# An expert loop whose passes pack several experts into one tile: two passes of three experts become one of two and one of four, which stands last

## The chip, the core and the metric

The kernel runs on one core of one Trainium2 chip. The metric is the device time of one execution in microseconds; the shown times are three runs of the same kernel. A profile of one further execution was taken by the hardware profiler.

## What is computed

The reference is one inference step of a small trunk of two layers over 128 context tokens and 128 sample tokens, 256 in all, each of width 1024, in float32. Each layer has a mixer (layer 0 a bidirectional linear recurrence, layer 1 differential attention) and then a mixture of 64 experts, of which each token takes 8. An expert is three matrices, gate and up of 1024 x 256 and down of 256 x 1024, 1 MB each. Only the mixture matters here:

```python
scores = jax.nn.sigmoid(x @ router)                     # (tokens, 64)
combine = ...                                           # top 8 of 64, 0 for the others
h = jax.nn.silu(jnp.einsum('btd,edf->btef', x, w_gate)) * jnp.einsum('btd,edf->btef', x, w_up)
routed = jnp.einsum('btef,efd->btd', h * combine[..., None], w_down)
shared = (jax.nn.silu(x @ ws_gate) * (x @ ws_up)) @ ws_down
return routed + shared
```

## The kernel before

**Passes.** All 64 experts of a layer are loaded, and the tokens that chose an expert are gathered for it. One pass of TensorE handles 128 gathered token slots, which are four lanes of 32. The string `ORDER` (line 54) says how the 26 passes of a loop split their lanes, and `SUBS` (line 59) which lane belongs to which expert of the pass. In a pass A two experts have two lanes each, in a pass B three experts have two, one and one, in a pass D two experts have three and one. The experts of a layer are numbered 0 to 63 in the order in which the passes consume them; `FIRST` (line 60) holds the first number of each pass. Experts 0 to 5 are fixed, the others are ordered on the chip by how many tokens they have, so that those with more tokens fall on more lanes; `column_ranks` (line 69) makes the table for that. What doesn't fit an expert's lanes is done by extra items, after pass 17.

**One pass** (`one_pass`, line 1387). TensorE does the gate and up products (`pass_gate_up`, or two halves one after the other in the first passes and in the last one), the scatter of the pass before, the transposes of the hidden rows, the gather for the pass after, the down product and the turning of the slots. All matmuls go through the helper `mm` and have its line, 889, in the profile. ScalarE takes the SiLU of the gate half (line 1872) when the gate and up products are done. VectorE and ScalarE copy between them. The gate and up products of a pass with lanes of 64 issue half as many matmuls as those with lanes of 32.

**Buffers.** SBUF has six places for a gate and up pair (`GATE_SLOTS`) and five for a down matrix (`DOWN_SLOTS`), line 49. Expert n uses the place `gate_of(n)` (line 468, in turns of six from expert 5 on) and the place n mod 5 for its down matrix. A place is refilled as soon as the expert that used it is done: `GATES_FREED` and `DOWNS_FREED` (lines 477 and 479) list, for each pass, the later experts whose place it frees.

**Loads.** SyncE issues them all, into one queue, in the order of its program. `refill(L, p)` (line 595) waits until the gate and up products of pass p are done (`gu_done`), issues the gate and up loads of the experts that take over its gate places, waits until the down product is done (`down_done`) and issues the down loads. The experts of the last pass, `END_EXPERTS` (line 481), are an exception: first the gate halves of all of them are issued, on the semaphore `end_gate_loaded`, then the up halves on the place's own semaphore (lines 615 to 622). In the last pass (line 1392) TensorE waits for all gate halves, does the gate half of the products, waits for the up halves and does the other half. Its wait counts `END_PLACES` (line 65), the gate places of the last pass. After the refills SyncE issues the load of the residual's gains and then, behind the first loop, the weights of the next stage.

**The end of the loop before the change**, with numbers of experts:

| pass | kind | experts | gate and up loads it sets free | down loads it sets free |
|---|---|---|---|---|
| 16 | B | 39, 40, 41 | 45, 46, 47 | 44, 45, 46 |
| 17 | A | 42, 43 | 48, 49 | 47, 48 |
| 22 | D | 54, 55 | 60, 61 | 59, 60 |
| 23 | A | 56, 57 | 62, 63 | 61, 62 |
| 24 | B | 58, 59, 60 | none | 63 |
| 25 | B | 61, 62, 63 | none | none |

The rest of a layer's mixture (the routing and its plan, the shared expert, the residual) is not touched. The first layer has no extra item in this run, the second has one, between passes 17 and 18.

Of the kernel before, what the change touches and what calls it, by code (L numbers as in the profile page):

```python
# [33 lines left out]
D = 1024  # L34
# [13 lines left out]
RING = 4  # L48
# [2 lines left out]
DOWN_LOADS = (E - RING) // DOWN_SLOTS + 1  # L51
STATIC = GATE_SLOTS
PLACED = RING + 1
ORDER = "AA" + "BABABDBA" + "BABABDBA" + "BABADABB"
ROUND = 8
PASSES = len(ORDER)
COLS = 4 * PASSES
ITEMS = COLS + 2 * XITEMS
SUBS = {"A": (0, 0, 1, 1), "B": (0, 0, 1, 2), "D": (0, 0, 0, 1)}
FIRST = [sum(SUBS[q][-1] + 1 for q in ORDER[:p]) for p in range(PASSES)]  # L60

SHARED_GATE, SHARED_UP, SHARED_DOWN = 4, 8, (12, 14)
MIDDLE = PASSES - ROUND
HALVED, EXTRAS = 5, 5
END_PLACES = (RING + 1, 2, 3)
FIRST_HALVES = 4

def column_ranks():

    n_big = ORDER.count("D")
    n_mid = ORDER.count("B") + 2 * ORDER.count("A") - STATIC
    big = iter(range(STATIC, STATIC + n_big))
    mid = itertools.chain(range(STATIC), range(STATIC + n_big, E))
    small = iter(range(STATIC + n_big + n_mid, E))
    lanes = []
    for kind in ORDER:
        if kind == "A":
            lanes.append([(next(mid), 2), (next(mid), 2)])
        elif kind == "B":  # L80
            lanes.append([(next(mid), 2), (next(small), 1), (next(small), 1)])
        else:
            lanes.append([(next(big), 3), (next(small), 1)])
    return [(rank, block) for places in lanes for rank, blocks in places for block in range(blocks)]
# [46 lines left out]
def constants():  # L131

    c = np.zeros((P, C_N), np.float32)
    c[:, C_ID:C_ID + P] = np.eye(P)
    c[:, C_TRI:C_TRI + P] = np.triu(np.ones((P, P)))
    c[:, C_ONE:C_ONE + P] = 1.0
    c[:, C_IOTA:C_IOTA + 64] = np.arange(64)
    c[:, C_E] = np.arange(P)
    c[:, C_EPS] = EPS
    for i in range(NS * MOD_MOST):  # L140
        c[i::32, C_SEL + i] = 1.0
    for i, (rank, block) in enumerate(column_ranks()):
        c[:, C_RANK + i], c[:, C_PLACE + i] = rank, -1.0 - 32 * block
    c[:, C_KEY] = E - 1 - np.arange(P)
    c[0:STATIC, C_KEY] = 1e5 * (STATIC - np.arange(STATIC))
    c[:, C_STEP:C_STEP + 4] = SLOTS * np.arange(4)
    pairs = HD // 4
    freqs = (10000.0 ** (-np.arange(pairs, dtype=np.float32) / pairs)).astype(np.float32)
    t = np.arange(P)
    ar = (t // 64).astype(np.float32)[:, None] * freqs  # L150
    ac = (t % 64).astype(np.float32)[:, None] * freqs
    c[:, C_COS:C_COS + HD] = np.concatenate([np.cos(ar), np.cos(ar), np.cos(ac), np.cos(ac)], 1)
    c[:, C_SIN:C_SIN + HD] = np.concatenate([-np.sin(ar), np.sin(ar), -np.sin(ac), np.sin(ac)], 1)
    return c
# [46 lines left out]
def slot_value(n):  # L201

    start = 48 * [q for _, q in PROLOGUE].count(n % RING)
    expert = [e for n0 in N_EXPERT for e in range(n0, n0 + RING * GATE_LOADS)]
    halved = [n0 + RING * (GATE_LOADS - 1) + q for n0 in N_EXPERT for q in END_PLACES if q < RING] + \
        list(range(N_EXPERT[1], N_EXPERT[1] + FIRST_HALVES))
    whole = tuple(range(N_QKV, N_QKV + 6)) + tuple(range(N_WO, N_WO + 4))
    return start + sum(16 if m in halved else 32 if m in expert else 48 if m in whole else 0 for m in range(n % RING, n + 1, RING))  # L210

def trunk(nc, a, outs, gains):
    y_prompt, y_sample, new_state, new_k, new_v = outs
    ctx = ExitStack()
    with ctx:
# [241 lines left out]
        def experts_of(p):  # L458
            return list(range(FIRST[p], FIRST[p] + SUBS[ORDER[p]][-1] + 1))

        def id_column(n):

            p = max(p for p in range(PASSES) if FIRST[p] <= n)
            return 4 * p + SUBS[ORDER[p]].index(n - FIRST[p])

# [31 lines left out]
        def gate_value(L, q, times):  # L497
            if q < RING:
                return slot_value(N_EXPERT[L] + q) + 32 * times
            return 32 * ((GATE_LOADS - 1) * L + times + 1) - 16 * L * (q in END_PLACES)  # L500

        def lanes(p, place_of):

            kind = ORDER[p]
            cut = (0, 64, 128) if kind == "A" else (0, 32, 64, 96, 128)
            return [(lo, hi - lo, place_of(experts_of(p)[SUBS[kind][lo // 32]])) for lo, hi in zip(cut, cut[1:])]

# [379 lines left out]
        def _(eng):  # L887
# [290 lines left out]
            def half_gate_up(j, half, places, done, within=None):  # L1178

                for k in range(KD):  # L1180
                    for lo, n, q in places:
                        at = 2048 * half + F * k
                        ins = mm(PS[lo:lo + n, 6, F * half:F * (half + 1)], xg[:, k, lo:lo + n],
                                 gate_place(q)[:, at:at + F], k == 0, k == KD - 1)
                    if within and k == 3:
                        within()
                if done:
                    ins.then_inc(done, 1)
# [48 lines left out]
            def moe(L):  # L1237
# [149 lines left out]
                def one_pass(p):  # L1387
# [4 lines left out]
                    if not more:  # L1392
                        eng.wait_ge(s.xg_act, j + 1)
                        eng.wait_ge(s.xg_dve, j + 1)
                        eng.wait_ge(s.end_gate_loaded, 16 * len(END_PLACES) * (L + 1) + 16)
                        half_gate_up(j, 0, lanes(p, gate_of), None)
# [1430 lines left out]
```

## Time and profile before

| | |
|---|---|
| three runs | 1354.79, 1354.95, 1357.23 us; median 1354.95 |
| the profiled execution | 1353.37 us, of which the span 1351.5 |
| TensorE matmul busy | 1293.1 us, 96% of the span |
| VectorE, ScalarE busy | 463.6 us (34%), 344.5 us (25%) |
| bytes moved by DMA | 507.94 MB, 376 GB/s over the span |
| chain of work that ended last | TensorE 87%, DMA 5%, VectorE 4%, ScalarE 2% |
| granted TensorE clock, mean | 0.988 |

### The profile page before, as it was taken

What the parts mean: (1) busy time and instruction counts of PE and PEld (TensorE: products, weight loads), DVE (VectorE), ACT (ScalarE), POOL (GpSimd) and SP (SyncE); (2) the same over time, 40 slices, a digit from 0 to 9 for tenths busy, and PEclk for the clock granted to TensorE, in tenths of its full rate; (3) what the DMA queues carried; (4) which work ended last, traced back from release to release, by engine and by line L of the source; (5) the groups of instructions that cost most, each with busy time, mean ns of one, the idle gap of its engine ahead of it and who ended that gap; (6) DMA issues with size and microseconds to landing.
All of it is one profiled execution on the core that took longest, in us unless ns stands there. A gap on an engine that the chain in (4) does not pass through costs nothing.

```text
span 1351.5 us, 24835 instructions
## 1 busy us (share of the span) xinstructions
PE 1293.1 (96%) x10046; PEld 682.7 (51%) x10046; DVE 463.6 (34%) x1188; ACT 344.5 (25%) x712; POOL 18.2 (1%) x23
## 2 busy tenths in 40 slices
PE   7989998999999999899989999899999999979997
PEld 5757646565454443344534454565645444444443
DVE  2556625323232223222231253632232322222223
ACT  2168033212212212122230243522121212212222
POOL 2100000000000000000000000000000000000000
PEclk9999999999999999899999999999999999999999
DMA  9896899999999999999999556889999999999996
GB/s 346 225 351 244 326 373 414 368 419 413 420 420 421 420 420 420 419 421 419 415 391 341 201 212 263 316 345 422 413 419 421 420 420 420 421 420 419 420 420 250
DMA packets 114514, 507.94 MB, mean 376 GB/s; under 512 B 19036, under 2 KB 27424, under 8 KB 64352
## 3 DMA queue, kind: packets, MB, share of 16 engines
q1 hardware_dynamic: 113136, 503.42, 92.8%
q0 software_dynamic: 1008, 2.45, 0.6%
q8 instruction: 83, 1.36, 0.4%
q10 hardware_dynamic: 256, 0.45, 0.1%
q14 instruction: 31, 0.25, 0.0%
HBM read 504.15 MB, written 2.14 MB: 375 GB/s over the span
## 4 chain that ended last, share of the span: by engine, by line
PE 87%; DMA 5%; DVE 4%; ACT 2%; issue 1%; SPq 0%; DVEq 0%; ACTq 0%
PE PS L889 84%; DMA W<-in_moe_w_up 2%; DMA ring<-in_moe_w_up 2%; DVE W L2262 1%; DMA ring<-in_mod_w 1%; PE PS L1194 1%; DMA ring<-in_moe_w_down 1%; PE PS L897 1%; DVE x L2137 0%; PE PS L1282 0%; DVE hT L2097 0%; PE PS L1521 0%; ACT W L1831 0%; ACT W L1830 0%; DVE W L2259 0%
## 5 line engine op out<-in xcount | busy, mean ns | idle before, releaser
L889 PE MATMUL PS<-ring,W 128*32 128x512 f32 (+5 forms) x3176 | 600.4, 537 | 1.5 <-DMA ring<-in_moe_w_down 0.8
L889 PE MATMUL PS<-W 128*128 128x128 bf16 (+7 forms) x3466 | 555.8, 360 | 4.6 <-DVE ring L2270 2.3
L889 PEld LDWEIGHTS PS<-W 128*128 128x128 bf16 (+4 forms) x3466 | 257.8, 110 | 129.7 <-issue 105.9
L889 PEld LDWEIGHTS PS<-ring,W 128*32 128x32 f32 (+2 forms) x3176 | 202.2, 121 | 196.3 <-issue 173.7
L889 PE MATMUL PS<-W,junk 128*128 128x128 bf16 x848 | 117.6, 221 | 7.3 <-issue 4.0
L889 PE MATMUL PS<-diag,W 128*128 128x512 bf16 (+2 forms) x424 | 114.8, 399 | 4.8 <-ACT diag L1887 2.2
L2393 DVE TENSOR_TENSOR diag<-PS,diag 128x512 f32<-128x512 f32 x100 | 69.1, 691 | 144.4 <-ACT diag L1885 144.4
L2387 DVE COPY W<-PS 128x512 f32<-128x512 f32 x53 | 36.6, 691 | 238.6 <-PE PS L889 238.6
L889 PE MATMUL PS<-ring,hT 128*128 128x512 f32 x256 | 115.5, 601 | 0.4 <-ACT hT L2028 0.3
L1885 ACT CAST diag<-PS 128x512 bf16<-128x512 f32 x100 | 58.5, 585 | 190.8 <-PE PS L889 190.8
L2370 DVE SCALAR_TENSOR_TENSOR W<-W,PS 128x256 f32<-128x256 f32 x52 | 25.0, 480 | 217.0 <-ACT W L1872 217.0
L1872 ACT ACTIVATE W<-PS 128x256 f32<-128x256 f32 x52 | 19.9, 383 | 287.4 <-PE PS L889 287.4
L889 PEld LDWEIGHTS PS<-W,junk 128*128 128x128 bf16 x848 | 67.1, 98 | 19.5 <-issue 6.9
L889 PE MATMUL PS<-hT,ring 128*128 128x256 f32 x320 | 73.5, 389 | 2.2 <-DVE hT L2097 2.2
L889 PEld LDWEIGHTS PS<-diag,W 128*128 128x128 bf16 (+2 forms) x424 | 38.8, 103 | 73.0 <-issue 46.3
L889 PEld LDWEIGHTS PS<-ring,hT 128*128 128x128 f32 x256 | 47.4, 192 | 55.4 <-issue 54.6
L889 PEld LDWEIGHTS PS<-hT,ring 128*128 128x128 f32 x320 | 61.1, 194 | 16.7 <-issue 5.9
L1880 ACT COPY W<-PS 128x512 f32<-128x512 f32 x53 | 31.1, 586 | 142.4 <-PE PS L889 142.4
L2398 DVE TENSOR_TENSOR rows<-diag 128x1024 bf16<-128x1024 f32 x50 | 61.3, 1226 | 9.6 <-ACT diag L1887 8.4
L1887 ACT CAST diag<-diag 128x1024 bf16<-128x1024 f32 x50 | 52.3, 1046 | 37.9 <-DVE diag L2393 37.9
L889 PE MATMUL PS<-rows,W 128*128 128x512 bf16 x200 | 60.4, 384 | 1.0 <-DVE rows L2398 1.0
L889 PE MATMUL PS<-ring,condT 128*32 128x512 f32 (+1 forms) x400 | 43.9, 564 | 0.2 <-DMA ring<-in_mod_w 0.2
(284 smaller groups left out, 858.0 us busy)
## 6 DMA issues: line engine op xcount, KB each, us to landing
ring<-in_moe_w_down SPq DMA_DIRECT2D x104, 1024.0 KB, 19.6
ring<-in_moe_w_gate SPq DMA_DIRECT2D x88, 1024.0 KB, 17.5
ring<-in_moe_w_up SPq DMA_DIRECT2D x88, 1024.0 KB, 20.8
W<-in_moe_w_gate SPq DMA_DIRECT2D x40, 1024.0 KB, 16.3
W<-in_moe_w_up SPq DMA_DIRECT2D x40, 1024.0 KB, 19.5
W<-in_moe_w_down SPq DMA_DIRECT2D x25, 1024.0 KB, 17.9
ring<-in_mod_w SPq DMA_DIRECT2D x28, 768.0 KB, 9.0
ring<-in_mod_w SPq DMA_DIRECT2D x16, 1024.0 KB, 12.2
```

Source lines behind the costliest of these rows:

```text
L889: return eng.matmul(out, lhsT, rhs, start=first, stop=last, skip_group_check=True)
L897: ins = eng.transpose(PS[:, norm_bank(n, b), i * P:(i + 1) * P], junk2[:, st, k * P:(k + 1) * P], ident)
L1194: ins = eng.transpose(PS[:, 7, fc * P:(fc + 1) * P], hE[:, fc * P:(fc + 1) * P], ident)
L1872: eng.activation(sg, PS[:, 6, 0:F], ACT.Silu).then_inc(sg_.silu_ready, 1)
L1880: eng.copy(xg[:, 0:4, :].rearrange("p k n -> p (k n)"), PS[:, 6, :]).then_inc(sg_.xg_act, 1)
L1885: eng.copy(oparts[0][:, half * 512:(half + 1) * 512], PS[:, 4 + half, :]).then_inc(sg_.o_act, 1)
L1887: eng.copy(oparts[1], orest).then_inc(sg_.o_act, 1)
L2262: ins = eng.scalar_tensor_tensor(out=y, in0=xpad[:, c, :, t:t + P], scalar=conv_w(t, c), in1=y, op0=ALU.mult, op1=ALU.add)
L2370: eng.scalar_tensor_tensor(out=hE.rearrange("p (c q) -> p c q", c=2), in0=sg.rearrange("p (q c) -> p c q", c=2), scalar=wslot[:, 0:1], in1 ...
L2387: eng.tensor_copy(xg[:, 4:8, :].rearrange("p k n -> p (k n)"), PS[:, 7, :]).then_inc(sg_.xg_dve, 1)
L2393: eng.tensor_tensor(orest[:, cols], PS[:, 4 + half, :], oparts[0][:, cols], ALU.subtract)\
L2398: eng.tensor_tensor(oparts[2], orest, oparts[1], ALU.subtract).then_inc(sg_.o_dve, 1)
```

## The change

The order of a loop changes at two passes: pass 16 goes from B to A, the last pass 25 from B to a new kind C with one expert for each lane. The table of ranks and the list of the last pass's gate places follow.

```diff
-ORDER = "AA" + "BABABDBA" + "BABABDBA" + "BABADABB"
+ORDER = "AA" + "BABABDBA" + "BABABDAA" + "BABADABC"
...
-SUBS = {"A": (0, 0, 1, 1), "B": (0, 0, 1, 2), "D": (0, 0, 0, 1)}
+SUBS = {"A": (0, 0, 1, 1), "B": (0, 0, 1, 2), "D": (0, 0, 0, 1), "C": (0, 1, 2, 3)}
...
-END_PLACES = (RING + 1, 2, 3)
+END_PLACES = (1, RING + 1, 2, 3)
...
             lanes.append([(next(mid), 2), (next(small), 1), (next(small), 1)])
+        elif kind == "C":
+            lanes.append([(next(small), 1) for _ in range(4)])
```

Each expert from number 41 on moves to a later place in the passes, and with it the loads that it sets free:

| pass | kind | experts | gate and up loads it sets free | down loads it sets free |
|---|---|---|---|---|
| 16 | A | 39, 40 | 45, 46 | 44, 45 |
| 17 | A | 41, 42 | 47, 48 | 46, 47 |
| 22 | D | 53, 54 | 59, 60 | 58, 59 |
| 23 | A | 55, 56 | 61, 62 | 60, 61 |
| 24 | B | 57, 58, 59 | 63 | 62, 63 |
| 25 | C | 60, 61, 62, 63 | none | none |

The numbers of passes, lanes, matrices and bytes are the same.

## Rows read from the trace of the kernel before

**Rows 1.** The page: DMA rate in 40 slices of the span, about 34 us each.
```profile
GB/s 346 225 351 244 326 373 414 368 419 413 420 420 421 420 420 420 419 421 419 415 391 341 201 212 263 316 345 422 413 419 421 420 420 420 421 420 419 420 420 250
```
**Rows 2.** The chain in order of time, first loop: start us, us, what.
```profile
626.10 25.41 DMA ring<-in_moe_w_up
```
**Rows 3.** Busy time in windows of one pass: length, engines busy, clock, DMA share, GB/s.
```profile
641.90:658.80 16.90, 16.57 (x147) 7.77 (x148) 4.98 (x11) 3.58 (x7) 0.00 (x0) 1.00 1.01 421
1163.60:1180.50 16.90, 16.44 (x131) 7.84 (x130) 4.98 (x11) 3.56 (x6) 0.00 (x0) 1.00 1.01 419
1301.20:1317.70 16.50, 16.50 (x147) 7.37 (x148) 4.98 (x11) 3.56 (x7) 0.00 (x0) 1.00 1.01 420
```
**Rows 4.** Timeline of ScalarE: SiLU of passes 24, 25 (first layer), 24 (second).
```profile
658.78 0.38 ACT L1872 ACTIVATE W<-PS 128x256 f32<-128x256 f32 x1 [5.27 <-PE PS L889]
675.25 0.38 ACT L1872 ACTIVATE W<-PS 128x256 f32<-128x256 f32 x1 [4.90 <-PE PS L889]
...
1317.69 0.38 ACT L1872 ACTIVATE W<-PS 128x256 f32<-128x256 f32 x1 [4.89 <-PE PS L889]
```
**Rows 5.** Line 586, first layer, pass 23's four half loads: issues and time to landing.
```profile
L586 SPq DMA_DIRECT2D ring<-in_moe_w_gate x2: 333/335/337, 642.1 to 642.6; - x2
...
L586 SPq DMA_DIRECT2D ring<-in_moe_w_up x2: 377/2331/4285, 643.0 to 643.5; - x2
...
DMA to landing us min/median/max: 20.2/24.8/27.9
```
**Rows 6.** Line 579, first layer, the last three down loads (652.7, 653.3, 668.7).
```profile
L579 SPq DMA_DIRECT2D ring<-in_moe_w_down x3: 332/338/346, 652.7 to 668.7; - x3
...
DMA to landing us min/median/max: 10.1/21.1/23.1
```
**Rows 7.** Line 579, second layer, the last three down loads (1311.7, 1312.2, 1327.6).
```profile
L579 SPq DMA_DIRECT2D ring<-in_moe_w_down x3: 332/332/333, 1311.7 to 1327.6; - x3
...
DMA to landing us min/median/max: 8.9/19.9/21.9
```
**Rows 8.** Timeline of TensorE, pass 25 in both layers: first gate product, down product.
```profile
668.08 0.41 PE L889 MATMUL PS<-ring,W 128*32 128x256 f32 x2
...
678.93 3.64 PE L889 MATMUL PS<-ring,W 128*32 128x512 f32 x32 [0.84 <-DMA ring<-in_moe_w_down]
...
1326.98 0.41 PE L889 MATMUL PS<-ring,W 128*32 128x256 f32 x2
...
1336.93 3.64 PE L889 MATMUL PS<-ring,W 128*32 128x512 f32 x32
```
**Rows 9.** Line 579, pass 17's last down load in the first and second layer.
```profile
L579 SPq DMA_DIRECT2D ring<-in_moe_w_down x1: 4952/4952/4952, 541.9 to 541.9; - x1
...
DMA to landing us min/median/max: 28.6/28.6/28.6
...
L579 SPq DMA_DIRECT2D ring<-in_moe_w_down x1: 333/333/333, 1200.6 to 1200.6; - x1
...
DMA to landing us min/median/max: 27.7/27.7/27.7
```
**Rows 10.** Timeline of SyncE: pass 18's first load in both layers.
```profile
560.75 0.34 SPq L576 DMA_DIRECT2D ring<-in_moe_w_gate  x1
...
1220.06 0.33 SPq L576 DMA_DIRECT2D ring<-in_moe_w_gate  x1
```
**Rows 11.** DMA issues outside the loops: count, KB each, median us to landing.
```profile
ring<-in_attn_w_o SPq DMA_DIRECT2D x4, 512.0 KB, 3.6
...
out<-x SPq DMA_DIRECT2D x2, 512.0 KB, 2.6
```
**Rows 12.** Busy time in windows: three stretches with idling, TensorE's busy time first.
```profile
98.60:103.80 5.20, 3.38 (x19) 2.96 (x16) 0.90 (x3) 4.52 (x10) 0.00 (x0) 1.00 1.03 384
688.70:691.40 2.70, 0.01 (x1) 0.00 (x0) 2.60 (x5) 2.15 (x4) 0.60 (x1) 1.00 1.05 385
691.40:694.80 3.40, 3.38 (x16) 3.16 (x16) 2.66 (x8) 2.01 (x7) 0.63 (x2) 0.50 1.05 387
```

## The prediction, made before the change ran

> **What bounds the kernel now.** I read the page first, then the chain of waits, then the last passes of each expert loop. In the slices of the page [rows 1] each loop moves 413 to 421 GB/s in most of its slices. The chain is mostly TensorE, with a few loads in it; one of these links is 25.4 us long [rows 2], but a link's length is the time from issue to landing, not idle time. So two things are full at once, and the question is which one ends last, and where. The windows of single passes show how long TensorE really stood still: 16.90 - 16.57 = 0.3 us in pass 24 of the first layer, 16.90 - 16.44 = 0.5 us in pass 17 of the second; pass 23 to 24 of the second has none (16.50 of 16.50), and all three run at 419 to 421 GB/s with a DMA share of 1.01 [rows 3]. TensorE needs 16.4 us for a pass, the loads arrive just in time, and neither has slack to give.
>
> The end of a loop then follows from the load queue. In the first layer pass 24's gate and up products end at 658.8 [rows 4]. Pass 23 had issued its two gate halves and two up halves from 642.1 on; the first landed at 642.1 + 20.2 = 662.3, the last, expert 63's up half, at 643.5 + 27.9 = 671.4 [rows 5]. The three last down loads, of experts 61 to 63, landed at 652.7 + 21.1 = 673.8, 653.3 + 23.1 = 676.4 and 668.7 + 10.1 = 678.8 [rows 6]: 2.5 us each, so the queue never ran dry although it was fed only 10 us ahead. In the second layer the last one landed at 1327.6 + 8.9 = 1336.5 [rows 7]. TensorE begins pass 25 at 668.08 and 1326.98, and its down product at 678.93 (after a wait for that load) and 1336.93 (no wait) [rows 8]; from begin to down product a pass without a wait takes 1336.93 - 1326.98 = 9.95 us.
>
> **What the change does to this.** Loads, bytes, lanes (104) and blocks for each rank stay the same, so the extra items do too. From pass 16 on, every pass up to 24 consumes one expert fewer by its end, so each refill from pass 16 to 23 issues three loads later than before. Pass 24 now frees a gate place that is still wanted. Its refill issues expert 63's gate half and up half when its own gate and up products end, and the down loads of 62 and 63 after its down product. Before, only one down load stood there.
>
> *Pass 16 becomes lanes of 64.* It issues 48 matmuls fewer a layer. The window with 131 matmul rows has 16.44 us busy, the one with 147 has 16.50 [rows 3]: 0.06 us for 16, under 0.2 us for 48, and it ends in the wait below. I cost it at nothing. The last pass had four lanes of 32 before and has them now: nothing. Passes 17 and 24 lose waits of 0.5 and 0.3 us; that too runs into the wait.
>
> *The last pass of the first layer.* The queue is full and in order, so its end, 678.8, stays, and I count back from it. The last four loads are now gate 63, up 63, down 62, down 63. Three of them take 678.8 - 671.4 = 7.4 us, so gate 63 lands at 671.4 [rows 5, 6]. It is issued at 658.8 with 10 us of loads ahead of it, so the queue has work throughout. TensorE starts 0.13 us after a landing (678.80 to 678.93 [rows 6, 8]): 671.5 instead of 668.08, 3.4 us later. Up 63 lands 2.5 us behind, inside the first half of the products (half of 675.25 - 668.08 [rows 4, 8], 3.6 us), so there is no second wait. The down product begins at 671.5 + 9.95 = 681.5, past the last landing; the old wait for it, 0.9 us, is gone. Net 681.5 - 678.9 = **2.5 us**. Queued behind TensorE's wait are the scatter of pass 24, the SiLU of pass 25 and the residual, so all of it shows. SyncE itself does not wait longer: the gains and the next stage's weights follow down 63 in the queue, whose time does not move.
>
> *The last pass of the second layer.* 1336.5 - 7.4 = 1329.1, plus 0.13, against 1326.98: 2.3 us; here no old wait is given back. To this comes a restart. Pass 17's last load landed at 1200.6 + 27.7 = 1228.3 [rows 9], and pass 18 issued its first at 1220.06 [rows 10]: 8.2 us ahead. With three loads (7.4 us) fewer in the queue that is 0.8 us, or 1.3 us with pass 17's 0.5. No row shows the start of a load on an empty queue; the nearest are the 512 KB transfers outside the loops, 2.6 and 3.6 us from issue to landing [rows 11]. At 420 GB/s 512 KB take 1.25 us, which leaves 1.4 to 2.3 us of delay. The queue therefore stands still for 0.1 to 1.0 us (zero, if the landing itself makes up most of that delay). I take 0.5: **2.8 us**. In the first layer 541.9 + 28.6 = 570.5 against 560.75 [rows 9, 10] leaves 9.7 - 7.4 = 2.3 us ahead, no less than the longest delay, so nothing.
>
> *TensorE's clock.* The last pass now follows 3.4 and 2.8 us (3.3 with the earlier arrival) without matmuls. The trace has two neighbours: in a stretch with 5.20 - 3.38 = 1.8 us of idling the granted clock stayed at 1.00, after 2.7 us of idling it stood at 0.50, the 1.2 GHz level, for the next 3.4 us [rows 12]. A stretch of 3.4 us at half speed does 1.7 us less work. That is the upper bound of its price, and zero the lower; both new waits are longer than the one of 2.7, so I take **1.7 us each, 3.4**.
>
> Sum: 2.5 + 2.8 + 3.4 = 8.7 us. The profiled execution took 1353.37 us (span 1351.5 and 1.9 around it), so it would take 1362.1. The median of the runs is 1354.95, 1.6 above that execution; the sum on the median gives **1363.6 us**.
>
> One row could be read another way. Of pass 23's four loads the first landed 9.1 us ahead of the last, where three even steps make 7.4: as if the first load behind a down load came 1.6 us early [rows 5]. Gate 63 would then land at 669.8 and up 63 would bind: half 1 starts at 674.0 instead of 671.6, and with the old 0.9 given back 1.5 us remain, 1.7 in the second layer; 3.2 in all, with waits too short for the clock. But those two gate halves share one semaphore, and all loads with one of their own came 2.5 apart [rows 6], so I take the even step. The Trainium skill (DMA: Bandwidth & Descriptors, Why a DMA increments its semaphore by 16 and not by 1) says that the engines of a transfer finish independently and that, with two in flight on one semaphore, early engines of the later one can fill the count. The even 2.5 us of the single loads [rows 6] agree with it. By that rule the early landing is only a count, and the sum is 8.7; taken as a landing it is 3.2.
>
> **Rivals.**
> - *The clock stays up.* For: the 1.8 us row. Against: both waits exceed the 2.7 us row. 2.5 + 2.8 = 5.3: 1360.2. Chance 0.18.
> - *The first load comes early*, as just worked out: 1358.2. Chance 0.08.
> - *The queue runs dry at pass 18 in earnest.* If the restart costs 2.3 us beyond the cover in the second layer and 1 us in the first, 2.8 more than I take: 1366.4. Against: 8.2 and 9.7 us were ahead before [rows 9, 10]. Chance 0.07.
> - *Not slower.* Passes 17 to 24 need one expert less each, TensorE runs ahead and the last pass finds its loads. Its place is the wait ahead of pass 25; it decides if gate 63 lands by 668.1, at most 9.3 us after its issue instead of 12.6, for which the queue would need 3.3 us of slack. Then only the 0.5 us of the second layer is won (the first still ends by its last down load): 1354.4. For: loads stand on the chain [rows 2]. Against: no pass in [rows 3] moves less than 419 GB/s. Chance 0.12.
>
> **How the numbers follow.** The forecast keeps 0.55. Low end: the early landing, 1358.2, less 0.2 of spread between runs: 1358.0. High end: the forecast with a restart of 1.0 (0.5 more) and one more half-speed stretch (1.7): 1365.8, and 1 us of spread: 1366.8. That leaves out the last rival and little else. 0.2% is 2.7 us, about what a measurement of this kernel can tell. Slower by more: forecast and the first three rivals, 0.88, less 0.02 for the early landing: 0.86. Of the last rival 0.03 might reach beyond 0.2% faster; the rest is 0.11.
>
> **What would show it.** Right: in pass 25 of both layers TensorE waits for a gate load issued at the end of pass 24's gate and up products, 3 to 4 us; the granted clock is 0.50 behind it; the down loads cause no wait; the last load lands within 1 us of the old distance from the loop's begin; passes 17 to 24 stand at 16.4 us. Wrong: a stretch in the loop under 415 GB/s, no wait ahead of pass 25, or a full clock behind the wait.

## The result, and the profile after

The changed kernel took 1366.99 us in the median of four runs (1363.71 to 1369.94), the kernel before 1354.87 beside it: a ratio of 1.0090, 95% interval 1.0074 to 1.0106, 12.1 us slower. The forecast was 8.7 us slower, 1363.6, with a range up to 1366.8: the direction was right, the size too small, and the range missed by 0.2 us. The profiled execution was the longest of the four, 1369.94 us with a span of 1368.1, 16.6 more than the span before. A second profile, of a later run of the same kernel (r8 below), had 1366.68 and 1364.9 (+13.4). So 12 to 17 us have to be found; what is read from one profile is the price in that execution, and the medians decide how much of it is usual.

The page's slices of the DMA rate after:

```profile
GB/s 348 216 356 244 329 373 398 394 421 413 421 419 421 421 420 419 414 420 420 413 383 298 157 253 248 342 346 422 413 420 419 421 420 421 420 310 402 420 420 234
```

Against [rows 1] the first loop looks the same. The second has a hole: 310 and 402 in slices 36 and 37, where before nothing in the loop was under 413. That is the first thing to follow up. ScalarE's SiLU of each pass marks how far TensorE has come. Its timeline after, first layer passes 24 and 25, then second layer passes 17, 18, 24 and 25:

```profile
655.17 0.38 ACT L1874 ACTIVATE W<-PS 128x256 f32<-128x256 f32 x1 [4.89 <-PE PS L891]
680.87 0.38 ACT L1874 ACTIVATE W<-PS 128x256 f32<-128x256 f32 x1 [14.14 <-PE PS L891]
...
1184.77 0.38 ACT L1874 ACTIVATE W<-PS 128x256 f32<-128x256 f32 x1 [4.88 <-PE PS L891]
1231.14 0.38 ACT L1874 ACTIVATE W<-PS 128x256 f32<-128x256 f32 x1 [11.76 <-PE PS L891]
...
1328.92 0.38 ACT L1874 ACTIVATE W<-PS 128x256 f32<-128x256 f32 x1 [4.89 <-PE PS L891]
1350.71 0.38 ACT L1874 ACTIVATE W<-PS 128x256 f32<-128x256 f32 x1 [10.24 <-PE PS L891]
```

The kernel before, second layer, passes 17 and 18:

```profile
1180.55 0.38 ACT L1872 ACTIVATE W<-PS 128x256 f32<-128x256 f32 x1 [5.38 <-PE PS L889]
...
1219.91 0.38 ACT L1872 ACTIVATE W<-PS 128x256 f32<-128x256 f32 x1 [9.54 <-PE PS L889]
```

Before, pass 25 of the first layer stood at 675.25 and pass 24 of the second at 1317.69 [rows 4]. So pass 25 of the first layer comes 5.6 us later; pass 0 of the second comes 4.7 later, and so it stays to pass 16. Between passes 17 and 18 of the second lie 46.4 us, before 39.4: **7.0 us that the forecast did not have**. Passes 18 to 24 keep their old distances, 11.2 us late. Pass 25 adds 5.3 more (21.8 us from pass 24's SiLU instead of 16.46).

TensorE's timeline shows what it waited for at these three places:

```profile
671.43 0.61 PE L891 MATMUL PS<-ring,W 128*32 128x256 f32 x1 [6.91 <-DMA ring<-in_moe_w_gate]
...
1215.22 0.28 PE L891 MATMUL PS<-W,junk 128*128 128x128 bf16 x2
1218.38 0.38 PE L891 MATMUL PS<-W 128*128 128x128 bf16 x4 [2.89 <-issue]
...
1342.09 0.61 PE L891 MATMUL PS<-ring,W 128*32 128x256 f32 x1 [3.82 <-DMA ring<-in_moe_w_gate]
```

And the windows around them (length, engines' busy time from TensorE on, granted clock, DMA share, GB/s):

```profile
664.50:671.40 6.90, 0.02 (x2) 0.01 (x1) 2.78 (x7) 1.46 (x2) 0.00 (x0) 0.84 1.01 419
671.40:676.10 4.70, 4.67 (x46) 2.48 (x49) 0.00 (x0) 0.00 (x0) 0.00 (x0) 0.50 1.01 419
...
1215.30:1218.30 3.00, 0.19 (x4) 0.07 (x2) 0.00 (x0) 0.00 (x0) 0.00 (x0) 1.00 1.02 418
1218.80:1225.60 6.80, 5.93 (x44) 3.31 (x45) 2.07 (x7) 0.58 (x1) 0.00 (x0) 0.50 0.52 216
1338.20:1342.00 3.80, 0.07 (x2) 0.00 (x0) 2.78 (x7) 1.52 (x2) 0.00 (x0) 0.96 1.01 423
1342.00:1345.00 3.00, 2.91 (x28) 1.57 (x32) 0.00 (x0) 0.00 (x0) 0.00 (x0) 0.50 1.01 421
```

The first and the last line of the timeline are the forecast wait for expert 63's gate half, with DMA at full rate and a clock of 0.50 behind it. The middle one is new. In the gather ahead of pass 18 TensorE stands still for 2.9 us ("issue": it waited for nothing that the profile shows), and then runs 6.8 us at half clock. In the same stretch the DMA share falls to 0.52: pass 18 comes too late to feed the load queue.

The load queue itself, from the lines of SyncE's issues: pass 17's last down loads, pass 18's first gate load, and the second layer's last two down loads, each with the time to landing:

```profile
L581 SPq DMA_DIRECT2D ring<-in_moe_w_down x2: 831/1400/1969, 1197.6 to 1198.6; - x2
...
DMA to landing us min/median/max: 25.4/26.1/26.8
...
L578 SPq DMA_DIRECT2D W<-in_moe_w_gate x1: 333/333/333, 1231.3 to 1231.3; - x1
...
DMA to landing us min/median/max: 5.1/5.1/5.1
...
L581 SPq DMA_DIRECT2D ring<-in_moe_w_down x2: 333/333/333, 1339.4 to 1339.9; - x2
...
DMA to landing us min/median/max: 7.6/8.6/9.6
```

1198.6 + 26.8 = 1225.4: all that was queued had landed 5.9 us before pass 18 issued its first load at 1231.3. That load landed 5.1 us later on an empty queue. The last one landed at 1339.9 + 9.6 = 1349.5 against 1336.5 [rows 7], 13.0 later: the 4.7 with which the layer began, and 8.2 lost here.

In the first layer nothing of this shows. There pass 18 came 3.2 us *earlier* than before, and the last down load (666.1 + 12.6 = 678.7) landed where it had (678.8 [rows 6]):

```profile
L581 SPq DMA_DIRECT2D ring<-in_moe_w_down x2: 333/335/337, 665.6 to 666.1; - x2
...
DMA to landing us min/median/max: 10.6/11.6/12.6
```

TensorE's wait is 6.9 us and not 3.4 because it arrives earlier, not because the load comes later.

### The profile page after: what moved, and what is told of

Same layout as the page of the kernel before. It is cut to its first block, busy times and chain, and to the rows that moved or that the text cites. A ratio compares the mean times of both kernels' runs of the same rounds, so it can differ in the third digit from the quotient of the medians.

```text
span 1368.1 us, 24593 instructions
## 1 busy us (share of the span) xinstructions
PE 1291.0 (94%) x9902; PEld 681.0 (50%) x9950; DVE 463.7 (34%) x1188; ACT 344.3 (25%) x712; POOL 18.2 (1%) x23
## 3 DMA queue, kind: packets, MB, share of 16 engines
q8 instruction: 82, 1.34, 0.4%
## 4 chain that ended last, share of the span: by engine, by line
PE 89%; DVE 5%; DMA 3%; ACT 2%; issue 2%; ACTq 0%; SPq 0%; DVEq 0%
PE PS L891 86%; DMA ring<-in_moe_w_gate 2%; DVE W L2264 1%; PE PS L1196 1%; DVE x L2139 0%; DMA rows<-in_norm_g 0%; PE PS L899 0%; DVE hT L2099 0%; PE PS L1523 0%; ACT W L1833 0%; ACT W L1832 0%; DVE W L2261 0%; DVE W L2389 0%; PE PS L1005 0%; DVE W L2737 0%
## 5 line engine op out<-in xcount | busy, mean ns | idle before, releaser
L891 PE MATMUL PS<-W 128*128 128x128 bf16 (+7 forms) x3290 | 561.6, 355 | 9.7 <-issue 6.4
L891 PEld LDWEIGHTS PS<-ring,W 128*32 128x32 f32 (+2 forms) x3256 | 205.5, 122 | 225.4 <-issue 198.5
L891 PE MATMUL PS<-diag,W 128*128 128x512 bf16 (+2 forms) x376 | 103.8, 399 | 12.4 <-issue 7.6
L891 PE MATMUL PS<-ring,condT 128*32 128x512 f32 (+1 forms) x400 | 44.7, 573 | 0.0
```

The source lines that it names most:

```text
L891: return eng.matmul(out, lhsT, rhs, start=first, stop=last, skip_group_check=True)
```

## The experiments

The theory from these readings: the change costs a wait and a half clock in each last pass, as forecast, and in the second layer a stall that comes from where TensorE's code lies, which makes pass 18 late while the queue has no cover left (cover is the time by which the next load is issued before the last one queued has landed). Rivals: the last pass is all of it; the stall was chance; the shorter cover costs the 8 us by itself.

The table gives what the kernels showed. "Stall" is TensorE's "issue" gap in or just behind the gather of pass 18 in the second layer; "17 to 18" the distance of these two SiLU there; "waits" TensorE's idle time ahead of pass 25, first / second layer. "Kept" stands for transposes that fill that wait. Ratios are against runs of the kernel before on the same chip; its medians there lie between the two given.

| kernel | median us | ratio, interval | stall | 17 to 18 | waits |
|---|---|---|---|---|---|
| before | 1353.8 to 1355.3 | 1 | 0.3 | 39.4 | none / none |
| changed | 1366.99 | 1.0090, 1.0074–1.0106 | 2.9 | 46.4 | 6.9 / 3.8 |
| r8, changed again | 1367.59 | 1.0092, 1.0079–1.0105 | 1.3 | 42.1 | 5.6 / 3.9 |
| e1, four experts at pass 18 | 1370.68 | 1.0121, 1.0102–1.0140 | 2.9 | 45.1 | none / none |
| e2, lag from pass 20 | 1359.73 | 1.0038, 1.0025–1.0051 | 0 | 39.3 | 2.7 / 1.9 |
| e3, clock kept (60, 34) | 1360.25 | 1.0039, 1.0027–1.0051 | 0 | 38.8 | kept |
| e4, pass 16 in four lanes | 1364.10 | 1.0071, 1.0057–1.0084 | 0.5 | 41.1 | 4.7 / 3.8 |
| e5, code moved, longer jump | 1371.18 | 1.0125, 1.0107–1.0142 | 4.2 | 46.4 | 6.9 / 3.9 |
| e6, before with code moved | 1358.03 | 1.0026, 1.0016–1.0035 | 3.0 | 43.7 | none / none |
| e7, e3 with the stall back | 1366.23 | 1.0089, 1.0075–1.0103 | 3.0 | 44.7 | kept |
| e8, clock kept (41, 34) | 1361.30 | 1.0042, 1.0026–1.0058 | 0 | 40.5 | kept |
| e11, before, gaps filled | 1356.03 | 1.0015, 1.0005–1.0026 | 0 | 39.0 | none / none |
| e12, changed, gaps filled | 1365.73 | 1.0086, 1.0072–1.0099 | 0 | 39.3 | 6.8 / 3.9 |

**e1: the pass of four experts in the middle.**

```
-ORDER = "AA" + "BABABDBA" + "BABABDAA" + "BABADABC"
+ORDER = "AA" + "BABABDBA" + "BABABDAA" + "CABADABB"
-END_PLACES = (1, RING + 1, 2, 3)
+END_PLACES = (RING + 1, 2, 3)
```

> The pass of four experts stands at pass 18 and the last pass has three experts again, so the expert lag of the change lasts only over passes 16 to 18. Theory (two costs: the last pass waits for one expert more, and in the second layer the queue of weight loads runs dry ahead of pass 18): the last pass's idle time goes back to what it was before in both layers, the dry queue at pass 18 of the second layer stays, with up to 8 us of the stream lost: 1355 to 1364 us, most likely 1360, the last load of the second layer landing up to 8 us later than before. Rival 1 (the last pass accounts for everything and the late pass 18 is made up): 1354 to 1356, as before. Rival 2 (the time goes to the changed number of items of pass 16, whatever the loads do): near the changed kernel, 1364 to 1368.

A miss on all sides: 1370.7. One part held: no wait ahead of pass 25 in either layer. But there are new ones in pass 19 (TensorE's timeline of e1, both layers):

```profile
585.84 6.49 PE L891 MATMUL PS<-ring,W 128*64 128x512 f32 x16 [5.52 <-DMA ring<-in_moe_w_down]
1257.56 5.15 PE L891 MATMUL PS<-ring,W 128*64 128x512 f32 x16 [5.55 <-DMA ring<-in_moe_w_down]
```

A pass of four experts frees four gate places at once. Its refill issues eight gate and up loads, 8 x 2.5 = 20 us of queue, ahead of the down loads of the next pass. In the first layer the first of the eight was issued at 559.3, TensorE wanted that down load at 580.3, and it landed at 585.7. So a pass of four costs 5.5 us in the middle too, by another wait. The stall is there as well, 2.95 us.

**e2: the lag moved behind pass 18.**

```
-ORDER = "AA" + "BABABDBA" + "BABABDAA" + "BABADABC"
+ORDER = "AA" + "BABABDBA" + "BABABDBA" + "BAAADABC"
```

> Pass 16 is as before and pass 20 takes the two experts instead, so that the lag lasts over passes 20 to 25 and the last pass keeps its four experts. Theory: the queue has its former cover at pass 18, first load of that pass within a microsecond of before, and only the last pass costs: some 4.7 us in the first layer and 4 to 5 us in the second, 1363 to 1365 us. Rival 1 (the last pass accounts for all of the change): 1366 to 1368, as the changed kernel. Rival 2 (the lag costs wherever it begins, by a dry queue at a later pass): over 1368.

1359.7, below every expectation: the last pass is not all of the change, and costs 5.4 us here, not 8 to 10. TensorE's timeline of e2 gives the forecast's own numbers:

```profile
671.50 0.38 PE L891 MATMUL PS<-ring,W 128*32 128x256 f32 x1 [2.66 <-DMA ring<-in_moe_w_gate]
...
1331.72 0.38 PE L891 MATMUL PS<-ring,W 128*32 128x256 f32 x1 [1.90 <-DMA ring<-in_moe_w_gate]
```

671.5 is to the tenth where the forecast had TensorE start. From there to the SiLU it took 680.36 - 671.50 = 8.86 us, before 675.25 - 668.08 = 7.17 [rows 4, 8]: 1.69 for one half-clock stretch of 3.4 us. In the second layer, after a wait of only 1.9, the clock stayed at 1.00. The SiLU, and the window behind the second wait:

```profile
680.36 0.38 ACT L1874 ACTIVATE W<-PS 128x256 f32<-128x256 f32 x1 [9.32 <-PE PS L891]
...
1331.70:1335.00 3.30, 3.28 (x63) 2.42 (x66) 1.40 (x3) 0.33 (x1) 0.00 (x0) 1.00 0.96 338
```

**e3 and e4: the clock kept, and pass 16 cut as before.** e3 adds transposes ahead of the last wait; e4 leaves pass 16's two experts in four lanes of 32, which gives TensorE its old 96 matmuls back and leaves the loads in the changed order.

```
 e3, one_pass, last pass:
+                        keep_clock(6, (60, 34)[L])
                         eng.wait_ge(s.end_gate_loaded, 16 * len(END_PLACES) * (L + 1) + 16)
 e4:
-            cut = (0, 64, 128) if kind == "A" else (0, 32, 64, 96, 128)
+            cut = (0, 64, 128) if kind == "A" and p != 16 else (0, 32, 64, 96, 128)
```

> The changed kernel with transposes into an unused bank of PSUM, 60 in the first layer and 34 in the second, while the last pass waits for its last expert's gate weights. Theory: the wait stays as long as it is (6.8 and 3.7 us), but the half clock after it (6.8 us from 669 and 3.4 us from 1342) goes, which gives back some 2.4 us in the first layer and 1.7 in the second: 1363 us against 1367. Rival 1 (what follows the wait is bound by the up and down loads that land later, not by the clock): 1366 to 1368, no change. Rival 2 (the transposes themselves run past the landing and delay the pass): over 1367.

> The changed kernel, with pass 16's down products and gates still cut in four parts of 32 slots as before, so that TensorE has the instruction count of before while the loads keep the order of the change. Theory (the second layer's loss at pass 18 comes from the shorter cover of the load queue, and the late pass 18 from TensorE's half clock and an instruction stall in the stretch of the extra items): no change beyond some tenths from the changed kernel, 1364 to 1369 us, with the same last landing of the load stream. Rival (the number and the place of the instructions make the stall of 2.9 us ahead of pass 18's gather): the stall is gone, pass 18 is 3 to 7 us earlier, 1359 to 1364 us.

e3 gained 6.7 us on the changed kernel (6.2 when each is taken against the kernel before on its own chip), more than any of its expectations, although its 60 transposes ran 2 us past the landing of the gate half (672.1) in the first layer. TensorE there, and the SiLU behind it:

```profile
667.53 6.75 PE L1005 MATMUL PS<-con 128*128 128x128 f32 x60
674.21 0.40 PE L891 MATMUL PS<-ring,W 128*32 128x256 f32 x1
...
681.39 0.39 ACT L1875 ACTIVATE W<-PS 128x256 f32<-128x256 f32 x1 [11.51 <-PE PS L891]
```

At full clock the products took 681.39 - 674.21 = 7.18 us, the 7.17 of before. But between the two profiles the larger part of the gain lies elsewhere: there is no stall at pass 18 in the second layer, and the distance of passes 17 to 18 is 38.8. The 60 transposes had moved all later code of TensorE by 120 instructions. e4 moved it by 192: the stall was 0.52, and 2.9 us of the time were gone (2.4 when each is taken against the kernel before on its own chip). The time lies where its two expectations meet; the stall, and pass 18 5.3 us closer to pass 17, are the rival's: the number and place of the instructions make the stall.

The place is counted in matrix products here as in the expectations: from the last eight products of the extra item, which TensorE still had to do when the jump was taken. In the changed kernel the stall stands behind the 28th; 20 of these belong to the gather, so "28 products into the gather", as some expectations have it, is 8 too many. In e4 it stands behind the 60th, past the gather.

**e5, e6, e7: the place of the code alone.** Transposes that are never run, in the code for a second extra item, which is jumped over since there is only one. They take no time and move what follows.

```
             with eng.If(count > 1):
+                for _ in range(skipped):
+                    eng.transpose(PS[:, 6, 0:P], ident, ident)
                 with eng.Fori(1, XITEMS) as i:
 second layer: e5 = changed + 60, e6 = before + 31, e7 = e3 + 68
```

> The changed kernel with 60 transposes added in TensorE's code for a second extra item of the second layer. With one extra item they are jumped over, never run; they only move all that follows by 120 instructions. Theory (the stall of 2.9 us ahead of pass 18's gather is TensorE waiting for its own next block of instructions after that jump, 28 matrix products behind the jump's target, and it brings two or three half-clock stretches with it): the stall is gone, pass 18 of the second layer runs 6 to 8 us earlier against its layer's start, the load queue there loses 1 to 3 us and not 8, 1359 to 1363 us. Rival 1 (the lateness of pass 18 is a chance of the clock, not of the code's place): 1364 to 1369, as the changed kernel. Rival 2 (the shorter cover of the load queue alone costs the 8 us): the same 1364 to 1369, with 7 to 9 us of the stream lost at pass 18 though the stall is gone.

> The kernel before, its order of experts untouched, with 31 transposes in the same place that is never run, which puts pass 18's gather of the second layer where the changed kernel has it against the blocks of 256 instructions (28 matrix products ahead of a block's end instead of 59). Theory: the stall of some 2.9 us appears in the kernel before, pass 18 comes 3 to 7 us later, and the passes after it are paced by TensorE, so that it stays in the end: 1357 to 1362 us against 1354.5. Rival 1 (the place of the code means nothing): 1353 to 1356. Rival 2 (the stall appears but the load queue's cover hides it): stall in the trace, 1354 to 1356.

> The run with the clock kept in the last pass, plus 68 transposes in the place that is never run, so that with the 60 of the first layer the code ahead of pass 18 of the second layer stands 256 instructions later, as in the changed kernel against its blocks. Theory: the stall of 2.9 us is back, pass 18 late by 5 to 7 us, and the time is the changed kernel's less what the half clock costs in the two last passes: 1363 to 1366 us, against 1360.3 without the stall. Rival 1 (the kept clock gave the whole gain of that run): 1359 to 1361. Rival 2 (the kept clock gives nothing): 1366 to 1368.

TensorE's timeline at the stall in the kernel before, r8, e4, e5, e6 and e7, in this order:

```profile
1212.54 0.17 PE L889 MATMUL PS<-W 128*128 128x12 bf16 x1 [0.28 <-issue]
```
```profile
1216.33 0.38 PE L891 MATMUL PS<-W 128*128 128x128 bf16 x4 [1.33 <-issue]
```
```profile
1216.92 0.62 PE L891 MATMUL PS<-W 128*32 128x512 f32 x2 [0.52 <-issue]
```
```profile
1218.49 0.28 PE L893 MATMUL PS<-W,junk 128*128 128x128 bf16 x2 [4.19 <-issue]
```
```profile
1211.76 0.50 PE L891 MATMUL PS<-W 128*128 128x128 bf16 x3 [2.98 <-issue]
```
```profile
1215.69 0.38 PE L893 MATMUL PS<-W 128*128 128x128 bf16 x4 [2.98 <-issue]
```

e6 is the cleanest: not one expert, lane or load differs from the kernel before, 31 products that are never run stand in the code, and the stall of 2.98 us appears, behind the 29th product where the 28th was expected; pass 18 comes 4.3 us later (SiLU of passes 17 and 18 in e6 below), and the median rises by 3.2 us. e7 brings it back to the 28th product and takes back 6.0 us of e3's gain (5.5 when each is taken against the kernel before on its own chip), 0.2 us above its range. e5 was a miss: the stall did not go, it moved ahead of the gather's first product and grew to 4.19, and the time, 1371.2, is the longest in the table.

```profile
1179.42 0.39 ACT L1874 ACTIVATE W<-PS 128x256 f32<-128x256 f32 x1 [5.53 <-PE PS L891]
...
1223.07 0.38 ACT L1874 ACTIVATE W<-PS 128x256 f32<-128x256 f32 x1 [10.19 <-PE PS L891]
```

The jump itself tells why. It is an instruction of its own on TensorE's sequencer ("PEldq" in the profile); its duration in ns and its start in the kernel before, the changed kernel, r8, e6 and e5, in this order:

```profile
L536 PEldq COMPARE_BRANCH  x1: 357/357/357, 1206.4 to 1206.4; - x1
```
```profile
L538 PEldq COMPARE_BRANCH  x1: 356/356/356, 1212.3 to 1212.3; - x1
```
```profile
L538 PEldq COMPARE_BRANCH  x1: 356/356/356, 1210.2 to 1210.2; - x1
```
```profile
L536 PEldq COMPARE_BRANCH  x1: 443/443/443, 1205.5 to 1205.5; - x1
```
```profile
L538 PEldq COMPARE_BRANCH  x1: 6081/6081/6081, 1212.4 to 1212.4; - x1
```

In e5 the jump took 6.1 us where it took 0.4 in the others: the longer jump had carried the target itself beyond what had been fetched. And the time from the jump to the end of the stall is the same wherever the stall stands:

| us | before | changed | r8 | e6 | e5 |
|---|---|---|---|---|---|
| from the jump until TensorE ran dry | 5.9 | 3.2 | 4.8 | 3.2 | 2.0 |
| stall | 0.3 | 2.9 | 1.3 | 3.0 | 4.2 |
| from the jump to the next product | 6.2 | 6.1 | 6.2 | 6.2 | 6.1 |

Over these stalls in all profiles and both layers it is 5.9 to 6.4 us. So the stall is what is left of some 6.1 us when TensorE has used up the products that it has behind the jump; the place of the code decides how many these are, and their pace (r8) counts too.

The trace shows the fetch itself. In a window of 1.6 us about the stall's begin in the changed kernel (1215.3 to 1216.9) the DMA view lists, beside the loads:

```profile
q8 instruction: 1, 0.02, 4.3%
```

On the page this queue has 82 transfers and 1.34 MB, 16 KB each. The one here started at 1215.86, 3.6 us after the jump and 0.4 us after TensorE had run dry, and TensorE went on 2.5 us after that start. In every profile one starts 3.5 to 3.8 us after the jump, with a stall or without. Counted from the shifts of these runs, a block holds 128 products with their weight loads: 28 - 96 + 128 = 60 in e4, 59 - 31 = 28 in e6. The Trainium skill (Runtime: NRT & Kernel Launch, Instruction fetch mechanics) says that an engine's instructions are refilled in blocks of 16 KiB, 256 instructions, that the next block is fetched in sequence, and that a taken branch to a target outside the blocks at hand forces a fetch first. The runs agree with it: all "issue" gaps of 1 us or more, in all profiles, stand behind the jump over the extra item's code, and in e5 the jump itself waited. That crossing a block's end is mostly hidden, as the Trainium skill also says there, did not hold here when the end came 28 products behind a jump.

**r8 and e8: the control, and the change without stall and half clock.** r8 is the changed kernel; e8 is e3 with 41 transposes in the first layer instead of 60.

> The changed kernel once more, beside the others on this chip. Theory (a stall fixed by where the code lies, with half-clock stretches that vary a little): 1366 to 1370 us, with a stall of 2.8 to 3.1 us 28 matrix products into pass 18's gather of the second layer. Rival (the stall and the late pass 18 were a chance of one profiled run): no such stall, 1360 to 1364.

> The changed kernel with 41 transposes in the first layer's last wait and 34 in the second's: what keeps the clock up, and moves the second layer's code by 82 instructions, so that the block's end lies 115 matrix products behind pass 18's start. Theory (the stall is gone, the two last waits remain as waits without a half clock; 60 transposes ran some 2 us past the landing in the first layer): 1358 to 1360 us, a little below the run with 60, and what is left above the kernel before, 4 to 5 us, is the two waits alone. Rival 1 (the stall comes back, because its place is not what was taken): 1364 to 1367. Rival 2 (the waits cost nothing once stall and half clock are gone): 1354 to 1356.

r8's time repeats to 0.6 us, and the stall stands at the same product, but it was 1.33 us long: a half-clock stretch from 1206.7 to 1213.5, across the jump, had made TensorE reach the block's end 4.8 us after the jump and not 3.2. Pass 18 was 2.7 us late and not 7.0; instead the second layer's last pass stood at half clock for 6.8 us and not 3.4. The sum comes out alike by other parts. e8, at 1361.3, lies just above its range and within 1.1 us of e3; both leave 5.9 to 6.0 us above the kernel before: the two waits, with neither stall nor half clock there. Some of it is not the waits: e3's transposes ran 2 us past the landing, and e8's load queue lost some 1.8 us at pass 18 of the first layer, where a stall of 4.5 us left it a cover of 2.3.

**e11 and e12: the same transposes between the layers in both orders.**

```
+            keep_clock(5, 24)            (ahead of norm_turn(2, b), about 691 us)
+                keep_clock(6, 22)        (ahead of turn_o(1), about 803 us)
 e11 (before) also: keep_clock(6, (14, 0)[L]) ahead of the extra items
```

> The kernel before with 24 transposes in the idle time ahead of 691 us and 22 ahead of 803 us, into banks of PSUM that are free there, and 14 ahead of pass 18 of the first layer, where the load queue has cover; 60 in all, so that the second layer's code stands where no block ends in pass 18's gather. Theory (a half-clock stretch costs where TensorE is awaited next): 1351 to 1353.5 us against 1354.9. Rival (the half clock comes back at another place of the stage between the layers, so filling two gaps gains nothing): 1355 to 1359.

> The changed kernel with the same 24 and 22 transposes between the layers and nothing else: the second layer's code moves by 92 instructions, the block's end lies some 110 matrix products behind pass 18's start, and the half clock behind the two last waits stays. Theory (stall and half clock are separate prices): no stall ahead of pass 18, half clock of 3.4 to 6.8 us in both last passes, 1361 to 1365 us against 1367.3 with the stall and 1360.3 to 1361.3 with neither. Against the kernel before with the same transposes it is 7 to 10 us longer. Rival (the half clock in the last passes costs nothing): 1359 to 1361.

e11 is 2.2 us above the kernel before, in its rival's range; what costs the 2.2 us is not shown. The half clock left 691 us and came at 804.6 in spite of the transposes. An earlier form, e10, with 14, 24 and 22 transposes at 46, 691 and 803 us, overwrote sums of the first stage and of the modulation that later products use; it took 1358.27, and its half clock came at 855.8 for 6.8 us.

> The kernel before with transposes into unused banks of PSUM in three idle places where its clock fell to half: 14 ahead of 46 us, 24 ahead of 691 us, 22 ahead of 803 us, 60 in all, which also takes the stall of 0.3 us out of pass 18 of the second layer. Theory (a stretch of 3.4 us at half clock costs up to 1.7 us where TensorE is what the next stage waits for): three stretches gone, 1350 to 1353 us against 1354.5. Rival 1 (those stages are bound by loads or by the other engines, and the half clock costs nothing there): 1354 to 1356. Rival 2 (the transposes run past the end of the waits or fall together with another stall of the code): over 1356.

e12 has the changed order, the two waits with the half clock behind them, and no stall. Its profiled execution took 1361.74 us, 8.4 above the profiled execution before; SiLU of pass 25 stood 8.3 us later in the span, where the forecast's sum was 8.7. But it was the shortest of its five runs. The other four took 1364.6 to 1366.6, three of them beyond the range, with granted clocks of 0.985 to 0.987 against 0.991: by 3.4 us at 0.50 for each stretch that is three to five half-clock stretches more, an estimate; where they lay no profile shows. The median of e12 is 11.9 us above the kernel before on its chip, as much as the changed kernel's 12.1. Only against e11, which has the same transposes, does it lie lower: the change costs 9.7 there, close to e4's 9.8.

## Why the prediction was right and wrong

*The last pass of the first layer: right.* TensorE was to start at 671.5 and started at 671.43; the queue's end stayed at 678.7; the down loads made no wait; the second layer began 4.7 us late (e12: 3.3) against 2.5 + 1.7 = 4.2. The wait itself was longer than written, 6.9 for 3.4, because pass 24 came 3.6 us earlier; an end set by the queue does not mind. The rival "the first load comes early" fell: gate 63 landed at 671.3, not 669.8.

*The clock: right in kind, somewhat low in size.* I took one stretch of 3.4 us in each layer, 1.7 each. From TensorE's start to the SiLU the surcharge over 7.17 us was 1.69 (e2, first layer), 2.3 (changed, first layer: 4.6 us of a 6.8 us stretch), 1.45 (changed, second), 2.1 and 1.7 (e12, first and second), 2.9 and 2.8 (r8, first and second: 1347.46 - 1337.47 - 7.17). In e3 it was zero. Two stretches in a row, as in the first layer of the changed kernel, r8 and e12 and in r8's second, stood in the high end of my range only.

*The restart of the second layer: the step that failed by its size.* "The queue therefore stands still for 0.1 to 1.0 us", and then "I take 0.5". Two things were mis-sized. The delay of a load on an empty queue was taken from 512 KB transfers outside the loops as 1.4 to 2.3 us; measured, a load lands 4.8 to 5.1 us after its issue on a queue that is empty (six profiles) or just running out (e8, e12), 2.3 to 2.6 us more than its step of 2.5. And the cover of 0.8 to 1.3 us was right only where pass 18 came in time. The table sets the stream lost (how much later than before the second layer's last load lands, less the layer's own shift at pass 0) against the time by which SyncE's first issue of pass 18 came after the last landing (a negative time is cover):

| | e12 | e8 | e4 | r8 | changed |
|---|---|---|---|---|---|
| issue after last landing, us | -1.2 | 0.0 | 0.5 | 1.6 | 5.9 |
| stream lost, us | 1.1 | 2.4 | 3.0 | 3.9 | 8.2 |

In these, each us of lateness costs a us, and 2.3 to 2.5 stand on top; e5 lost 8.3 at 5.9 in the same way, while e7 (7.6 at 4.2) and e1 (8.4 at 4.8) lost a us more, which stays open. e12's 1.1 is what the step should have had. The first layer's "nothing" for a cover of 2.3 us was luck: in the changed kernel pass 18 came early enough for 5.4, and where the cover was 2.3 and 1.8 (e8, e4) the queue lost some 1.8 and 1.5 there.

*Pass 16's lanes: the step that failed in kind.* Of the prediction's signs of being wrong one came, a stretch of the loop under 415 GB/s (310), and it stands where this step puts it. "It issues 48 matmuls fewer a layer", and then "I cost it at nothing". As engine time it is nothing. As code it moved the gather of pass 18 by 192 instructions in the second layer, so that a block's end fell 28 products behind a jump instead of 59. That made the stall of up to 2.9 us, shown by e6 and e7, where nothing but the place of the code differs. In all five profiles with a stall of 2.9 us or more (changed, e1, e5, e6, e7) a half-clock stretch began within 1.2 us of its end. And the late pass met a queue with its cover gone. Between the profiles of the changed kernel and e12, 46.4 - 39.3 = 7.1 of their 8.2 us lie between passes 17 and 18, 1.4 at the second layer's start, and the last pass gives 0.3 back. But these two are the longest execution of the one and the shortest of the other.

In medians, each taken against the kernel before on its own chip, the stall's price is smaller and less sharp: 2.4 and 2.5 us (changed and r8 against e4), 2.4 and 2.6 (against e12 less e11's 2.2), but 0.2 and 0.4 (against e12 as it stands); 3.2 (e6 against before); 5.4 and 5.5 (e7 against e8 and e3). Each kernel's own interval is 1.3 to 2.2 us either way, so the prices against e4 and e12 are not clear of noise, those of e6 and e7 are. The experiments fix its cause, not one price for it, since the half-clock stretches shift from run to run.

So the 12.1 us divide like this, in medians. Waits and restart without stall and half clock there leave 5.9 and 6.0 (e3, e8), where the forecast has 2.5 + 2.8 = 5.3. With the half clock it is 9.8 and 9.7 (e4, and e12 against e11), where the forecast has 8.7. The remaining 2.3 to 2.6 go with the stall, for which the forecast has nothing. Within the noise just given, that term is the largest part of the miss of 3.4.

Of the rivals, "the queue runs dry at pass 18 in earnest", chance 0.07, is what happened, with a price of 8 us in one profile and 4 in the other instead of its 2.8; the evidence that I set against it, 8.2 us of cover before, would be used up by the three loads, as the prediction's own sum had it. "Not slower" fell: TensorE did run ahead, by 3.6 us in the first layer, and only waited longer.

The same kind of stall had stood in the trace of before all along, 3.95 us ahead of pass 18 in the first layer, and the prediction says nothing of it. There it is harmless: the queue had cover, and its end did not move when the stall shrank to 2.8 after the change. What makes it harmless is the cover, and the change took that in the second layer.

## What to carry to other kernels

An edit that takes instructions away is not free because their time was small: it moves all later code, and behind a jump the engine may meet the end of what has been fetched; here it needed some 6 us of work in hand to hide that. Look for "issue" gaps right behind jumps, and test with instructions that are never run before blaming the edit. Count a queue's cover against the latest that its feeder may come, not against when it came in one profile, and price a load on an empty queue from its own kind: here some 2.4 us on top of its step, then a us for each us late. An order that ends a loop on more consumers of a full queue pays for the loads that now stand last, and for the half clock behind the wait, here 1.7 us for a stretch of 3.4 that falls wholly on work.

## What the hardware showed that was not expected

- TensorE's instructions arrive over a DMA queue of their own in transfers of 16 KB; behind a jump the profile shows waits of 0.3 to 4.2 us for them in the second layer and 2.1 to 5.4 us in the first, called "issue". The transfer starts 3.5 to 3.8 us after the jump, TensorE goes on 2.3 to 2.8 us after that start, and from the jump to the next product 5.9 to 6.4 us pass in all. A jump whose target was not there took 6.0 to 6.2 us itself (e5; the kernel before in its first layer, 6.06), the others that were taken 0.3 to 0.5.
- Half-clock stretches in these profiles are 3.4 or 6.8 us long, once 10.2 (the kernel before at 541.2; the one at the end of the span apart). Filling two gaps between the layers with transposes did not lessen them reliably: e11 still had one at 804.6, e10 got one of 6.8 us at 855.8.
